# Two implicit convolution filters in a two-block transformer kernel: the sums over the taps moved ahead of their norms, the skip row added to the sums, the second filter's frequency strips in another order, and the input's norm behind their evictions

## What is computed

```python
def hyena_filters(n, w1, b1, w2, b2, freq, w3):
    z = hyena_positional_features(n)
    hdn = jnp.sin(fr * (z @ w1 + b1))
    hdn = jnp.sin(fr * (hdn @ w2 + b2))
    filt = hdn @ w3
    decay = jnp.exp(-t * jnp.abs(deltas))
    return filt.reshape(n, HYENA_ORDER, 2, HYENA_WIDTH) * decay[:, None, None, :]

def bidir_long_conv(z, h_fwd, h_bwd, d_skip):
    taps = jnp.concatenate([h_fwd, jnp.zeros_like(h_fwd[:1]), h_bwd[:0:-1]], axis=0)
    taps = taps * lax.rsqrt(jnp.sum(taps * taps, axis=0, keepdims=True) + EPS)
    zf, tf = jnp.fft.rfft(z, n=2 * n, axis=1), jnp.fft.rfft(taps, n=2 * n, axis=0)
    y = jnp.fft.irfft(zf * tf[None], n=2 * n, axis=1)[:, :n]
    return y + z * d_skip

def modulated_norm(x, g, shift, scale):
    return rms_norm(x, g) * (1 + scale) + shift
```

## Time and profile before

| | |
|---|---|
| median of 3 runs | 2989.39 us (2987.66 to 2998.61) |
| the profiled execution's own time | 2984.14 us |
| its span, first to last instruction | 2982.3 us |
| TensorE busy with matmuls | 2835.1 us, 95% of the span |
| VectorE busy | 1564.1 us, 52% |
| ScalarE busy | 1026.4 us, 34% |
| GpSimd busy | 395.0 us, 13% |
| granted clock of TensorE, mean | 0.990 of full speed |

### The profile page before, as it was taken

The page is one execution under the profiler, slowest core; times in us unless marked ns, Lnnn a source line. Parts: engine busy times, 40 slices in busy tenths (PEclk is TensorE's granted clock), DMA queues, the critical chain, the costliest instruction groups (busy, mean ns, idle before and its releaser), DMA issues.

```text
span 2982.3 us, 40236 instructions
## 1 busy us (share of the span) xinstructions
PE 2835.1 (95%) x15815; PEld 2211.7 (74%) x15815; DVE 1564.1 (52%) x3045; ACT 1026.4 (34%) x1850; POOL 395.0 (13%) x513
## 2 busy tenths in 40 slices
PE   7899999999988999999999999999999999999998
PEld 3498865799964585677887788878566887788887
DVE  6735666846677546554235633435646325653344
ACT  2233244124256424544223432312554323332231
POOL 3300012420014321211110000000212011000000
PEclk9999999999999999999999999999999999999999
DMA  6533311042242142112232232333010333132332
GB/s 195 169 123 109 112 50 56 30 131 94 59 107 49 57 106 60 45 36 91 94 106 99 97 101 85 99 99 97 29 58 22 113 99 106 43 113 99 99 99 71
DMA packets 224931, 261.80 MB, mean 88 GB/s; under 512 B 12818, under 2 KB 187010, under 8 KB 224616
## 3 DMA queue, kind: packets, MB, share of 16 engines
q1 hardware_dynamic: 207328, 203.93, 21.9%
q0 software_dynamic: 12544, 45.08, 4.3%
q10 hardware_dynamic: 4872, 10.21, 1.6%
HBM read 245.04 MB, written 13.11 MB: 87 GB/s over the span
## 4 chain that ended last, share of the span: by engine, by line
PE 58%; DVE 6%; ACT 1%; issue 1%; DMA 0%; POOL 0%; SPq 0%; DVEq 0%; ACTq 0%; POOLq 0%
PE PS L359 32%; PE PS L3797 10%; PE PS L156 4%; PE PS L1235 3%; PE PS L1224 3%; PE PS L3694 2%; PE PS L1209 2%; DVE HL L302 1%; DVE S L1264 1%; DVE S L2668 1%; DVE S L2664 1%; DVE S L2693 0%; DVE S L2683 0%; PE PS L2506 0%; ACT HL L295 0%
## 5 line engine op out<-in xcount | busy, mean ns | idle before, releaser
L302 DVE TENSOR_TENSOR HL<-S,HL 128x2048 fp32r<-128x2048 f32 (+1 forms) x180 | 367.1, 2045 | 610.2 <-ACT HL L295 610.1
L295 ACT ACTIVATE HL<-S 128x2048 fp32r<-128x2048 f32 (+1 forms) x180 | 305.8, 1706 | 630.7 <-PE PS L359 281.7
L359 PE MATMUL PS<-xT,HL 128*128 128x512 f32 (+2 forms) x1920 | 436.8, 387 | 7.7 <-DVE xT L2518 4.7
L359 PEld LDWEIGHTS PS<-xT,HL 128*128 128x128 f32 (+1 forms) x1920 | 350.0, 186 | 88.5 <-DVE xT L2518 5.4
L359 PE MATMUL PS<-xT_up,HL 128*128 128x512 f32 (+1 forms) x1632 | 351.0, 377 | 1.7 <-DVE S L3810 1.7
L3797 PE MATMUL PS<-HL,hd 128*128 128x512 f32 x1536 | 350.1, 389 | 0.1
L359 PEld LDWEIGHTS PS<-xT_up,HL 128*128 128x128 f32 x1632 | 293.1, 188 | 58.5 <-issue 2.5
L3797 PEld LDWEIGHTS PS<-HL,hd 128*128 128x128 f32 x1536 | 288.0, 188 | 60.7 <-PE PS L3797 1.0
L1324 ACT ACTIVATE S<-S,S 128x256 f32<-128x256 f32 (+5 forms) x292 | 189.1, 648 | 165.4 <-DVE S L1264 157.7
L1360 POOL TENSOR_SCALAR S<-S,S 128x512 f32<-128x512 f32 (+4 forms) x216 | 146.4, 690 | 438.0 <-DVE S L1279 218.9
L1224 PEld LDWEIGHTS PS<-S,S 128*128 128x128 f32 (+1 forms) x1048 | 112.0, 139 | 120.6 <-issue 40.5
(11 more groups left out here) (422 smaller groups left out, 4094.8 us busy)
## 6 DMA issues: line engine op xcount, KB each, us to landing
S<-in_mlp_w_up SPq DMA_DIRECT2D x32, 1024.0 KB, 5.3
S<-in_mlp_w_down SPq DMA_DIRECT2D x32, 1024.0 KB, 4.9
...
```

The source lines that it names most:

```text
L295: m = a.activation(high, raw, ACT.Copy)
L302: m = v.tensor_tensor(low, raw, high.bitcast(F32), ALU.subtract)
L359: m = pe.matmul(dst, l[x], r[y], start=(i == 0 and j == 0), stop=(i == n - 1 and j == 2))
```

## The change

Five edits, all in the opening stage.

1. `tap_sums` is split in `tap_pairs` (one call for the differences, one for the sums), `tap_halves(x, part)` and `tap_eighths(x, part)` for a long filter, and `short_tap_sums`. They are made from the taps as they are, before `spread`: for order 0 the differences ahead of `tap_norm`, the sums and the halves of `d` ahead of `spread`; for order 1 both pairs right after the strips of `short0`. The last half of `s` and the eighths come after `spread`.
2. `spread` no longer relies on the sums being made afterwards: it adds the skip row to tap 0 and, in one more operation on one partition (two rows of 512), to the two sums of `s` that hold tap 0.
3. The strips of the long filters come in another order: 2, 0, 1, 3 for order 0 and 2, 1, 0, 3 for order 1. What each waits for follows: strip 2 waits for the row added to the sums, no longer for the halves.
4. `x.sums` is `T01[1][0:2]` for both orders, so order 1's sums lie where its own spectrum goes, and the wait at L1788 is gone. The strip order 2, 1, 0, 3 frees each quarter of the sums before the eviction that overwrites it.
5. `tn = normed(...)` comes after strips 0 and 3 of `long1`, no longer ahead of strips 1 and 3, and of the transposes that nobody reads (33, 33 and 28 of them) four are left, ahead of `long0`'s strip 2.

```diff
@@ -1464,7 +1464,7 @@
         x = Spectrum()
         x.o, x.nt, x.at, x.s, x.d, x.Tr, x.Ti, x.before = o, nt, at, s_, d_, Tr, Ti, before
         x.total, x.scale = ((sqa, sclA), (sqb, sclB))[nt == 2]
-        x.sums = T01[1 - o][0:2]
+        x.sums = T01[1][0:2]
         x.done = []
         return x
 
@@ -1537,6 +1537,7 @@
         act()
         pool()
         x.squared = sq_read[-1]
+        x.taken = squares[1][1]
 
     def tap_norm(x):
 
@@ -1565,8 +1566,11 @@
 
         b, b_row = bank(), bank()
         free, full, x.scaled = psum_free[b], mm.next(), ac.next()
-        row_free, row, x.spread = psum_free[b_row], mm.next(), dv.next()
-        psum_free[b], psum_free[b_row] = x.scaled, x.spread
+        row_free, row, row_read = psum_free[b_row], mm.next(), dv.next()
+        psum_free[b], psum_free[b_row] = x.scaled, row_read
+        added = dv.next()
+        x.spread = dv.next()
+        x.ready = {2: added} if x.nt == 4 else {0: added, 1: x.spread}
 
         def tensor():
             pe.wait_ge(*free)
@@ -1592,54 +1596,64 @@
             v.wait_ge(*ld_skip[x.o].all())
             v.wait_ge(*row)
             gain = x.total[0:1, :]
-            v.tensor_tensor(gain, PS[0:1, b_row, :], skip[x.o], ALU.mult).then_inc(*vl.step())
+            v.tensor_tensor(gain, PS[0:1, b_row, :], skip[x.o], ALU.mult).then_inc(*vl.event())
             v.wait_ge(*vl.at)
+            two = x.sums[0][0:1, 0:3:2, :] if x.nt == 4 else short_sums[0:1, 0:2, :]
+            v.tensor_tensor(two, two, bcast(gain, 1, 2), ALU.add).then_inc(*vl.event())
             v.tensor_tensor(x.s[0:1, 0, :], x.s[0:1, 0, :], gain, ALU.add).then_inc(*vl.event())
 
         tensor()
         act()
         dve()
 
-    def tap_sums(x):
-
-
-        x.ready = {0: dv.next()}
-        if x.nt == 2:
-            x.ready[1] = x.spread
-            x.y = []
-            if x.before:
-                v.wait_ge(*x.before.read)
-            v.wait_ge(*vl.at)
-            for i, z in enumerate((x.s, x.d)):
-                y0, y4 = short_sums[:, 2 * i, :], short_sums[:, 2 * i + 1, :]
-                v.tensor_tensor(y0, z[:, 0, :], z[:, 1, :], ALU.add).then_inc(*vl.step())
-                m = v.tensor_tensor(y4, z[:, 0, :], z[:, 1, :], ALU.subtract)
-                m.then_inc(*(vl.event() if i else vl.step()))
-                x.y.append({0: (y0, y4), 1: (z[:, 0, :], z[:, 1, :])})
-            return
-        x.ready[2] = x.ready[0]
-        x.ready[1], x.ready[3] = dv.next(), dv.next()
+    def short_tap_sums(x):
+
+        x.y = []
+        if x.before:
+            v.wait_ge(*x.before.read)
+        v.wait_ge(*x.taken)
+        v.wait_ge(*vl.at)
+        for i, z in enumerate((x.s, x.d)):
+            y0, y4 = short_sums[:, 2 * i, :], short_sums[:, 2 * i + 1, :]
+            v.tensor_tensor(y0, z[:, 0, :], z[:, 1, :], ALU.add).then_inc(*vl.step())
+            v.tensor_tensor(y4, z[:, 0, :], z[:, 1, :], ALU.subtract).then_inc(*vl.step())
+            x.y.append({0: (y0, y4), 1: (z[:, 0, :], z[:, 1, :])})
+
+    def tap_pairs(x, op):
+
+        at = 0 if op == ALU.add else 2
+        v.wait_ge(*x.taken)
+        v.wait_ge(*vl.at)
+        for z, u in ((x.s, x.sums[0]), (x.d, x.sums[1])):
+            v.tensor_tensor(u[:, at:at + 2, :], z[:, 0:2, :], z[:, 2:4, :], op).then_inc(*vl.step())
         x.y = [{0: (z[:, 1, :], z[:, 3, :]), 2: (u[:, 2, :], u[:, 3, :]), 1: (u[:, 1, :], u[:, 0, :]),
                 3: (z[:, 0, :], z[:, 2, :])} for z, u in ((x.s, x.sums[0]), (x.d, x.sums[1]))]
+
+    def tap_halves(x, part):
+
+        z, u = (x.s, x.d)[part], x.sums[part]
+        if part == 0:
+            x.ready[0] = dv.next()
         v.wait_ge(*vl.at)
-        for z, u in ((x.s, x.sums[0]), (x.d, x.sums[1])):
-            v.tensor_tensor(u[:, 0:2, :], z[:, 0:2, :], z[:, 2:4, :], ALU.add).then_inc(*vl.step())
-            v.tensor_tensor(u[:, 2:4, :], z[:, 0:2, :], z[:, 2:4, :], ALU.subtract).then_inc(*vl.step())
-            v.wait_ge(*vl.at)
-            v.tensor_tensor(z[:, 1, :], u[:, 0, :], u[:, 1, :], ALU.add).then_inc(*vl.step())
-            m = v.tensor_tensor(z[:, 3, :], u[:, 0, :], u[:, 1, :], ALU.subtract)
-            m.then_inc(*(vl.step() if z is x.s else vl.event()))
-        for n, (z, u) in enumerate(((x.s, x.sums[0]), (x.d, x.sums[1]))):
-            v.wait_ge(*vl.at)
-            v.scalar_tensor_tensor(u[:, 0, :], u[:, 1, :], -c8, z[:, 2, :], ALU.mult, ALU.subtract).then_inc(*vl.step())
-            v.wait_ge(*vl.at)
-            v.scalar_tensor_tensor(z[:, 2, :], u[:, 1, :], -c8, z[:, 2, :], ALU.mult, ALU.add).then_inc(*vl.step())
-            v.wait_ge(*vl.at)
-            m = v.scalar_tensor_tensor(u[:, 1, :], u[:, 3, :], c8, z[:, 0, :], ALU.mult, ALU.add)
-            m.then_inc(*(vl.event() if n else vl.step()))
-            v.wait_ge(*vl.at)
-            m = v.scalar_tensor_tensor(z[:, 0, :], u[:, 3, :], -c8, z[:, 0, :], ALU.mult, ALU.add)
-            m.then_inc(*(vl.event() if n else vl.step()))
+        v.tensor_tensor(z[:, 1, :], u[:, 0, :], u[:, 1, :], ALU.add).then_inc(*vl.step())
+        m = v.tensor_tensor(z[:, 3, :], u[:, 0, :], u[:, 1, :], ALU.subtract)
+        m.then_inc(*(vl.step() if part else vl.event()))
+
+    def tap_eighths(x, part, ready=False):
+
+        z, u = (x.s, x.d)[part], x.sums[part]
+        if ready:
+            x.ready[1], x.ready[3] = dv.next(), dv.next()
+        v.wait_ge(*vl.at)
+        v.scalar_tensor_tensor(u[:, 0, :], u[:, 1, :], -c8, z[:, 2, :], ALU.mult, ALU.subtract).then_inc(*vl.step())
+        v.wait_ge(*vl.at)
+        v.scalar_tensor_tensor(z[:, 2, :], u[:, 1, :], -c8, z[:, 2, :], ALU.mult, ALU.add).then_inc(*vl.step())
+        v.wait_ge(*vl.at)
+        m = v.scalar_tensor_tensor(u[:, 1, :], u[:, 3, :], c8, z[:, 0, :], ALU.mult, ALU.add)
+        m.then_inc(*(vl.event() if ready else vl.step()))
+        v.wait_ge(*vl.at)
+        m = v.scalar_tensor_tensor(z[:, 0, :], u[:, 3, :], -c8, z[:, 0, :], ALU.mult, ALU.add)
+        m.then_inc(*(vl.event() if ready else vl.step()))
 
     def strip(x, k, busy=0):
 
@@ -1748,21 +1762,26 @@
     tap(short0, 1)
     ada_step(0, 1, False)
     split_next()
+    tap_pairs(long0, ALU.subtract)
     tap_norm(long0)
     ada_step(0, 2, False)
     split_next()
+    tap_pairs(long0, ALU.add)
+    tap_halves(long0, 1)
     spread(long0)
-    tap_sums(long0)
+    tap_halves(long0, 0)
     ada_step(0, 3, False)
     tap_norm(short0)
-    strip(long0, 0, busy=33)
+    strip(long0, 2, busy=4)
     split_next()
-    strip(long0, 2)
+    tap_eighths(long0, 1)
+    tap_eighths(long0, 0, ready=True)
+    strip(long0, 0)
+    short_tap_sums(short0)
     spread(short0)
     ada_step(0, 4, False)
     split_next()
     strip(long0, 1)
-    tap_sums(short0)
     strip(long0, 3)
     ada_step(0, 5, False)
     split_next()
@@ -1772,6 +1791,8 @@
         tap(long1, t)
     strip(short0, 0)
     strip(short0, 1)
+    tap_pairs(long1, ALU.subtract)
+    tap_pairs(long1, ALU.add)
     ada_step(0, 6, False)
     split_next()
     store_spectrum(long0)
@@ -1784,26 +1805,28 @@
     ada_step(0, 8, False)
     t_mod = modulation(0)
     split_next()
+    tap_halves(long1, 1)
     spread(long1)
-    v.wait_ge(*ld_spill.all())
-    tap_sums(long1)
+    tap_halves(long1, 0)
+    tap_eighths(long1, 1)
+    tap_eighths(long1, 0, ready=True)
     ada_step(0, 9, False)
     tap_norm(short1)
-    strip(long1, 0, busy=33)
+    strip(long1, 2)
     split_next()
-    strip(long1, 2)
+    strip(long1, 1)
+    short_tap_sums(short1)
     spread(short1)
     ada_step(0, 10, False)
     split_next()
+    strip(long1, 0)
+    strip(long1, 3)
     tn = normed(X, sb(BIG + 17408, 1024), tx)
-    strip(long1, 1)
-    tap_sums(short1)
-    strip(long1, 3)
     ada_step(0, 11, False)
     split_next()
     store_spectrum(long1)
     for k in range(2):
-        strip(short1, k, busy=0 if k else 28)
+        strip(short1, k)
     for e in (pe, v, a, g):
         e.wait_ge(*ld_const.all())
     ada_fold()
```

## The result

The changed kernel takes 2975.8 us (median of 6 runs, 2969.0 to 2980.9) against 2990.1 for the kernel before in the same comparison (6 runs, 2985.0 to 2998.6): ratio 0.995 [0.9933, 0.9966], 10 to 20 us faster. The predicted time was 2979.0, the predicted difference -10.4. The profiled execution of after took 2977.42 us with a span of 2975.6; that of before, 2984.14 and 2982.3, was one of the quicker ones of its kernel, so the two spans differ by only 6.7 us.

What follows compares the result with a forecast made beforehand. TensorE was taken as the bound from 200 us on, VectorE as the chain from 100.4 to 146.3 us. With A's gain spent in B, 0.3 - 10.7 = -10.4 us, so 2989.4 became 2979.0 us; range 2970 to 2987.

Steps and rivals of the forecast that it cites:

- A: From the first norm to the last strip of `long0`: gains 3.7 us on TensorE, some 3 on VectorE.
- The new operation: The row's extra add to the sums, 1x2x512 on one partition: priced at 1.22 us, between 0.68 and 1.36.
- B: From there to the skip row of `long1`: A's gain is spent, row 0.3 us later (1.5 earlier to 4.4 later).
- the foreseen turns: In B, VectorE taking up to two turns with GpSimd's last additions for `long1`: adds 2.5 us.
- the slack of the chunk: In B, slack against the added time, since adaptive step 8 waited for its w_ada chunk before; no size given.
- C: VectorE's list from `long1`'s skip row to `short1`'s last eviction: 35.2 us instead of 45.9, 10.7 less.
- The wait for spectra: In C, VectorE's wait for stored spectra at 105.47 us goes away: 3.7 us.
- the squares: In C, VectorE's wait for ScalarE's squares of x at 129.65 us goes away, covered by evictions: 4.1 us.
- The dropped transposes: Unread transposes on TensorE in the opening: dropping them costs nothing in time and may cost clock.
- A's gain lives on through B: Rival, 15%: `long1`'s row comes 1.5 to 3 us earlier; gain 12.2 to 15, about 2976 us.
- The stores' collision: Rival, 20%: x's scalings take turns with GpSimd's `long1` store issues, 4.3 us and more return; about 2984 us.
- The clock rival: Rival, 4%: without transposes TensorE stays at half clock after 102 us, ending 6.8 us later; about 2996 us.

Runs made afterwards that it cites:

- Experiment 7: The changed kernel with only the two additions of `long1`'s pairs moved behind its norm, the differences left in place: 2970.0 us, ratio 0.9942.
- experiment 2: The kernel before with only the input's norm moved behind strips 1 and 3 of `long1`: 2984.5 us, ratio 0.9981.
- experiment 6: The changed kernel with `long1`'s four pairs behind its norm and the sums where the kernel before has them, with the wait for stores: 2985.3 us, one run.
- experiment 4: The changed kernel with the unread transposes put back (33, 33 and 28): 2975.4 us, ratio 0.9954.
- experiment 8: The changed kernel with only the 28 transposes ahead of `short1`'s first strip put back: 2972.2 us, ratio 0.995.
- experiment 1: The kernel before with only its 94 unread transposes taken out: 2991.2 us, ratio 1.0007.

## Why the prediction was near, and which step was off

The forecast was -10.4 us in the opening; measured, -13.4 at the table load and -13.6 at `short1`'s evictions. The mechanism and the stages were right; one term, A, was mis-sized by 2.7 us.

- **A: the term that was off.** "A gains 3.7 us on TensorE": it gained 6.5 (71.73 to 65.27; 0.2 to 0.4 of it is the earlier start of this execution). The spreading started at 41.39, not 42.5, since the norm's matmuls slipped by 0.7, not 1.1, and its small steps lost 0.6, not 1.3. The row's last matmul ended at 44.91, 3.5 after that start, where 3.9 was put down (46.4). And "TensorE has 3.9 us of adaptive step, fold, norm and four transposes" was too much: from 44.91 they took 2.8, since the clock had come back (the step's last 13 matmuls 1.03, against 1.85 in the kernel before; the norm's eight 128x1 matmuls 1.03, against 1.84 at 36.06; the four transposes 0.64). So strip 2 started at 47.74, not 50.3: 1.1, 0.4 and 1.1 us. VectorE would not have let it start sooner, as the row was added to the sums (L1602) until 47.69. The granted clock in stretches of 2 us, columns as in the earlier trace rows:

```profile
42.00:44.00 2.00, 2.00 (x11) 1.52 (x11) 1.90 (x3) 0.53 (x1) 0.00 (x0) 0.50 1.08 383
44.00:46.00 2.00, 2.00 (x25) 1.26 (x23) 1.97 (x4) 0.07 (x1) 0.00 (x0) 0.89 0.10 31
98.00:100.00 2.00, 2.00 (x23) 1.01 (x15) 1.80 (x2) 0.00 (x0) 0.00 (x0) 0.73 0.61 245
100.00:102.00 2.00, 2.00 (x12) 1.43 (x12) 1.97 (x4) 0.00 (x0) 0.00 (x0) 1.00 0.56 169
134.00:136.00 2.00, 1.51 (x8) 1.29 (x7) 1.91 (x4) 2.00 (x4) 1.32 (x3) 0.50 1.12 385
```

  It was back by 46 us. The text had itself noted that the clock was back by 46.9. Strip 1 followed at 58.16, not 60.6, and the last two strips took 7.11, not 7.4: with the 2.4 before them, 2.7 in all.
- **The new operation,** priced 1.22 between bounds of 0.68 and 1.36, took 1.21: in these rows an operation on one partition costs by its elements in a lane (1x512 0.67, 1x1024 1.21, 128x1024 1.22).
- **B** was to spend A's gain and 0.3 more. It spent 4.3 us, where 4.0 was forecast, so its price was right as a sum; but with 6.5 to spend from, L1599 came 2.2 earlier, not 0.3 later. The pairs were dearer than the 4.9 put down (7.00, the foreseen turns), and the slack of the chunk was really there: these two misses, in opposite directions, make the sum come out, which is luck. Experiment 7 recovers 1.8 us of the pairs' price.
- **C:** 35.2 us forecast for VectorE's list, 132.66 - 98.16 = 34.5 measured. The wait for spectra (3.70) and for the squares (4.08) went as forecast; experiment 2 prices the second by itself, and experiment 6 shows what the first becomes in the new order.
- **The dropped transposes "cost TensorE nothing in time"**: dropping `long1`'s 33 and `short1`'s 28 indeed moved nothing by time in the new order (experiments 4 and 8), but `long0`'s 33 would have held strip 2 and all behind it, some 2 us at `long1`'s skip row (experiment 4). In the old order dropping all 94 cost 3.5 us (experiment 1).
- **The rivals.** "A's gain lives on through B" had the right size (12.2 to 15, though a row 1.5 to 3 us earlier gives only 12.2 to 13.7) for a wrong reason: the pairs ran into GpSimd's additions and took 7.00, and no chunk paced step 8; the gain was there because A was larger. The stores' collision did not come: six scalings at 4.07 against 4.06, while the issues beside them stretched from 0.54 to 0.90 (one) and 0.67 (five). The Trainium skill (SBUF — State Buffer, 'The "DVE blocks DMA" trap') says that GpSimd can't write descriptors while VectorE runs a two-port fast-mode operation; in what mode the scalings ran no row shows, and here six of the eight issues were longer, by 1.0 us in all, and nobody waited for them. The clock rival needed a low clock until 137 us; it was 0.73 at 98 and 1.00 at 100 us (rows above), earlier than the 110 of the earlier trace rows.
- **The total.** 2979.0 forecast, 2975.8 measured. "Within 0.5%" was given 77%, and the gain of 0.5% lies on that line. With A at its measured size the same sum gives -13.1. The lower end of "5.9 to 12.9" is 5.6 by its own terms (10.7 - 4.4 - 0.7), which changes nothing else.

What stays open: why the stores of the spectra land later without the transposes in the old order, what the parts of edits 1 to 3 bring one by one, and what sets TensorE's speed in the stretches at 155 us and after 450 us.
